# Second stage of a hybrid layer pair: all eight PSUM banks in one pool, and first loads issued one stage earlier

## The chip, the cores and the metric

The kernel runs on one core of one Trainium2 chip. The metric is the device time of one execution in microseconds (us), the median of three runs; less is better. Everything is float32, with float32r (a replicated, reduced form of float32 that TensorE takes at full rate) in the large projections.

## The reference, cut to what matters

Two blocks run one after the other on 2048 positions of width 1024. The first block is where most of the change lies:

```python
def hybrid_layer(x, ...):
    p = rmsnorm(x, norm_g) @ w_in                       # one projection, 3076 columns
    p_shift, g_rwkv, q_down, kv_down, k_idx_raw, w_idx, g_attn = jnp.split(p, ...)
    y_rwkv = rwkv7_branch(p_shift, g_rwkv, ...)         # 8 heads of 64, a recurrence over time
    y_attn = dsa_branch(q_down, kv_down, k_idx_raw, w_idx, g_attn, ...)
    return x + concat(y_rwkv, y_attn) @ w_out

# in dsa_branch, for each block of 128 queries
score = einsum('bqh,bqhs->bqs', wi, relu(einsum('bqhd,bsd->bqhs', qi, k_idx)))   # index scores
_, idx = lax.top_k(score, 256)                          # the 256 best keys of each query
s = einsum('bqhr,bqkr->bhqk', qa, c_kv[idx]);  p = softmax(s);  o = einsum('bhqk,bqkr->bqhr', p, c_kv[idx])
```

The second block is dense attention with 12 heads (queries and keys of 64 plain and 32 rotated features), a small attention to 256 memory rows, gates and an output projection with its residual, and a last normalization.

## The kernel before, in words

**Stages.** The program has seven stages, each with one function for each queue (SP, PE, ACT, DVE, POOL): stage a (normalization, the first projection, the preparation of the recurrence, and the index search of four query blocks), stage 2 (the recurrence of RWKV and the sparse attention with the other searches), the first output projection (`mix1`), stage 4 (the second block's input projection), the heads stage (its head projections and the memory keys), stage 5 (dense attention) and the last output projection (`mix2`). `phase_end` (L342) parts them: each engine drains and signals, and waits for the other compute engines; only SP waits for all. The compute engines don't wait for SP.

**Orders.** In four of the stages the work is a list of pieces (`("score", b, x, n)` is one piece). The code of each engine is run once without a chip, and notes for each piece its waits, its signals and an assumed time for each instruction. `Order.settle` (L202) then plays the engines against each other: each engine has lanes whose pieces stay in order, and it takes the piece that could start first, and among equals the one that stands first in the list. The order that comes out is fixed in the program. On the chip every engine runs its pieces in that order, one by one: whatever stands behind a waiting instruction waits too.

**Stage 2.** It works on two things at once, woven by `weave` (L1415). The RWKV part has 16 turns of 128 positions: `gram` (two products of 64-row blocks), `lv0`, `lvy`, `lvl`, `lvu` (a triangular inverse in five levels, in tiles Xl, Xu, Y, Lm), `sm`, `sa`, `sb`, `sc` (the state's step), `gn0` to `gn2` (group normalization). The attention part has `kT` and `vv` (keys and values), `log` (index scores), `bit` and `flip` (a search for the 256th largest score, 31 steps for each block), `score`, `exp`, `pT` (the probabilities turned by TensorE), `pv`, `rb` and `fin`. Query blocks are taken in the order `BLOCKS` = (7, 6, 5, 4, 15, ..., 8, 3, 2, 1, 0); the first four are searched in stage a and their masks go out to DRAM and come back.

**PSUM in stage 2.** Each of the eight banks has a fixed use. Banks 4, 5 and 6 are a ring (`ring`, L1418): every `kT`, `vv`, `log`, `score` and `pT` piece gets the next one or two of them in the order of the list, and waits for the bank's last reader. Banks 0 and 1 hold `gram`, then `lvl` and `lvu`. Bank 2 holds `lv0`, `lvy`, `gn0`, `gn1`, `gn2` in turn (`b2_free`, L1436). Bank 3 holds the state's step, `sm` to `sc`. Bank 7 holds the attention's output of one pair of heads, from the first `pv` to `fin`:

```python
ring.setdefault(k, []).append((bank[4 + ring_n % 3], ring_last[ring_n % 3]))   # L1418 ff.
ring_last[ring_n % 3] = w
ring_n += 1
```

**Loads at the borders of stages.** `sp_a` (L768) issues at the piece of gate tile (7, 3) the loads of the latents, their two weights and the index keys (`ckvT`, traced as P, `pt`, `kidx`) for stage 2, into memory that the projection has left. All other loads of stage 2 are issued by `sp_2` (L1497) once `phase_end` has passed. `sp_heads` (L2732) issues the loads of head 0, first half (`load_heads(q, 0)`, L3054) for stage 5; `sp_5` (L3110) issues the second half, `load_heads(q, 1)`, after its border. ACT begins stage 5 with four instructions that zero rows of two query tiles (`zero_row`, L3091); a row of maxima, `mrow`, is later put in their place by DMA (`row_in`, L3079).

**Names of the profile.** L134 is `mm`, L137 `turn`, L144 and L145 `act`, L148 `tt`, L154 and L155 `ts`, L160 `stt`, L163 `copy`, L180 `addmax`, L128 `dma`. All eight banks bear the name psum.

## Time and profile before

| | us |
|---|---|
| median of three runs | 4168.22 (4159.9 to 4170.84) |
| the profiled execution, device time | 4170.54 |
| its span, first to last instruction | 4168.7 |
| mean granted TensorE clock | 0.970 |

| engine | busy us | share of the span |
|---|---|---|
| TensorE (PE) | 3868.3 | 93% |
| VectorE (DVE) | 2706.6 | 65% |
| ScalarE (ACT) | 2078.9 | 50% |
| GpSimd (POOL) | 1276.1 | 31% |

The last instruction of TensorE's part of stage a starts at 811.4 us; its first of stage 2 at 816.0, of `mix1` at 2022.1, of the heads stage at 2607.1, of stage 5 at 2822.8. Idle time is shown with what ended it, the last signal that came. The granted clock is given as a share of full speed.

### The profile page before, as it was taken

To read this page: it belongs to the slowest core of one execution; us is meant where nothing else is said; L and a number is where in the kernel's file an instruction comes from. 1 tells how busy PE (TensorE), PEld (TensorE's weight loads), DVE (VectorE), ACT (ScalarE), POOL (GpSimd) and SP (SyncE) were. 2 spreads that over 40 slices of the span, in tenths; PEclk is the share of its full clock that TensorE was granted. 3 is DMA by queue.
4 is the path that set the end of the run, shared out by engine and by line. 5 is a ranking of instruction groups with operands and counts; after the bars stand their busy time and mean duration, and the time that the engine had idled before them with its cause. 6 is when DMAs were issued, how large, how long until landed. Compare 5 with 4: busy or idle time off the path is not lost. (4 is left out here: it accounts for less than half of the span.)

```text
span 4168.7 us, 76113 instructions
## 1 busy us (share of the span) xinstructions
PE 3868.3 (93%) x31032; PEld 2729.3 (65%) x31032; DVE 2706.6 (65%) x5103; ACT 2078.9 (50%) x3089; POOL 1276.1 (31%) x1016
## 2 busy tenths in 40 slices
PE   6999989799888999898898999898999999999899
PEld 5777657566666766666686878774555555555477
DVE  6576778678767777888763332454777777776533
ACT  4354678678677877766333222223333333334421
POOL 2132123233544443553110000002454544545100
PEclk9999999899999999999899999998999999999899
DMA  3344223412211212122565344763232322321243
GB/s 119 93 127 144 83 96 104 144 45 52 59 35 39 54 44 53 44 58 73 162 217 197 109 143 145 251 216 74 58 88 57 79 57 60 86 57 39 94 144 111
DMA packets 389564, 407.29 MB, mean 98 GB/s; under 512 B 115936, under 2 KB 288416, under 8 KB 388960
## 3 DMA queue, kind: packets, MB, share of 16 engines
q1 hardware_dynamic: 388096, 399.00, 32.7%
q8 instruction: 244, 4.00, 0.5%
q10 hardware_dynamic: 1120, 3.45, 0.2%
q14 instruction: 104, 0.85, 0.1%
HBM read 249.87 MB, written 152.47 MB: 97 GB/s over the span
## 5 line engine op out<-in xcount | busy, mean ns | idle before, releaser
L144 ACT ACTIVATE PT<-psum 128x1024 f32<-128x1024 f32 x384 | 394.3, 1027 | 653.5 <-PE psum L134 652.9
L172 DVE TENSOR_REDUCE m<-psum 128x1 f32<-128x1024 f32 x384 | 468.6, 1221 | 286.9 <-PE psum L134 286.9
L134 PE MATMUL psum<-xc,wah 128*128 128x512 f32 x1600 | 528.7, 412 | 15.8 <-DVE xc L148 7.7
L148 POOL TENSOR_TENSOR part<-PT 128x1024 f32<-128x1024 f32 x144 | 341.6, 2372 | 474.3 <-DVE all L148 374.1
L148 POOL TENSOR_TENSOR Lm<-gm,cst 64x512 f32<-64x512 f32 x192 | 258.4, 1346 | 383.3 <-PE psum L134 192.8
L134 PE MATMUL psum<-PT,V 128*64 128x512 f32 x1536 | 371.5, 605 | 0.0
L134 PEld LDWEIGHTS psum<-xc,wah 128*128 128x128 f32 x1600 | 301.6, 192 | 94.5 <-issue 21.6
L134 PE MATMUL psum<-xc,wal 128*128 128x512 f32 x800 | 318.4, 398 | 0.0
L145 ACT ACTIVATE bias<-score,cand,cols 128x2048 bf16<-128x2048 f32 (+4 forms) x155 | 244.5, 1578 | 79.7 <-DVE cand L155 75.9
L145 ACT ACTIVATE sgn<-score,cand,cols 128x1920 bf16<-128x1920 f32 (+4 forms) x155 | 227.9, 1470 | 61.2 <-DVE cand L155 59.7
L134 PE MATMUL psum<-hc,w4h 128*128 128x512 f32 x800 | 249.0, 392 | 0.0
L137 PE MATMUL psum<-cst,P 128*128 128x128 f32 x1088 | 183.6, 293 | 41.8 <-DVE pt L163 27.8
L134 PE MATMUL psum<-m_wh,m_yh 128*128 128x512 f32 x512 | 203.1, 397 | 7.3 <-DVE m_wl L148 5.9
L134 PEld LDWEIGHTS psum<-PT,V 128*64 128x64 f32 x1536 | 93.3, 136 | 178.0 <-issue 177.7
L134 PE MATMUL psum<-m_wl,m_yh 128*128 128x512 f32 x512 | 201.5, 393 | 0.0
L134 PE MATMUL psum<-m_wh,m_yl 128*128 128x512 f32 x512 | 201.4, 393 | 0.0
L180 DVE CUSTOM_DVE_ANT_0 P<-psum,bias 128x512 f32<-128x512 f32 (+3 forms) x320 | 181.9, 605 | 26.9 <-PE psum L134 24.0
L137 PEld LDWEIGHTS psum<-cst,P 128*128 128x128 f32 x1088 | 119.1, 145 | 116.4 <-issue 45.8
L148 DVE TENSOR_TENSOR all<-all,part 128x1024 f32<-128x1024 f32 x144 | 192.1, 1334 | 4.2 <-POOL part L148 4.2
L148 POOL TENSOR_TENSOR all<-PT 128x1024 f32<-128x1024 f32 x48 | 114.6, 2388 | 255.0 <-ACT PT L144 255.0
L134 PE MATMUL psum<-KNh,QNh 64*128 64x512 f32 x768 | 174.6, 451 | 18.5 <-DMA QNh<-scr_qnh 11.4
L134 PEld LDWEIGHTS psum<-KNh,QNh 64*128 64x128 f32 x768 | 72.3, 185 | 181.4 <-DVE m L172 70.9
(391 smaller groups left out, 9038.0 us busy)
## 6 DMA issues: line engine op xcount, KB each, us to landing
raw_a<-in_w_a SPq DMA_DIRECT2D x50, 512.0 KB, 3.7
raw_w<-in_w_in SPq DMA_DIRECT2D x32, 512.0 KB
QNh<-scr_qnh SPq DMA_DIRECT2D x48, 256.0 KB, 4.9
QRh<-scr_qrh SPq DMA_DIRECT2D x96, 128.0 KB, 4.6
QNl<-scr_qnl SPq DMA_DIRECT2D x48, 256.0 KB, 6.2
xin<-in_x SPq DMA_DIRECT2D x16, 512.0 KB
scr_AR<-AR SPq DMA_DIRECT2D x32, 256.0 KB, 2.4
scr_BK<-BK SPq DMA_DIRECT2D x32, 256.0 KB, 2.2
```

The source lines that it names most:

```text
L134: return self.e.matmul(out, a, b, start=start, stop=stop, skip_group_check=True)
L137: return self.e.transpose(out, src, ident) if self.e else self.idle(0.17)
L144: return self.e.activation(out, src, f, bias=bias, scale=scale)
L145: return self.e.activation(out, src, f, bias=bias, scale=scale, accum_out=acc)
L148: return self.e.tensor_tensor(out, a, b, op) if self.e else self.vector(out)
L172: return self.e.tensor_reduce(out, a, AX, op, negate=negate) if self.e else self.vector(a)
L180: return self.e.tensor_tensor_reduce(out, a, b, 1.0, -3.0e38, ALU.add, ALU.max, acc)
```

## The change

In stage 2 no bank has a fixed use any more. A piece that needs banks claims them (`Desk.claim`), and names what will free them. `Order.settle` gives each claim the banks that are free first at the moment at which it places the piece in TensorE's order; a piece whose claim can't be met at all isn't placed yet. In the program the claim becomes a wait for the last reader of just these banks. The order of the banks given in follows from that play. Loads: AR and BK of turn 0 and the index queries of block 4 are now issued by `sp_a` at the piece (7, 3), with waits for their own stores; the tiles of stage 2 are laid out anew so that they fit. `pe_a` ends with a wait for the last two mask stores, and two DVE pieces of stage 2 wait for SP's end of stage a. The masks come back one by one with each block's queries. TensorE waits before the first `score` of a pair for the turned probabilities of two pairs ago and for the block's mask. In the heads stage SP's first piece is given 5 us in the play (no instruction), and SP also issues the high parts of `load_heads(q, 1)`. The zeroing of rows in stage 5 moves from ACT to POOL, and one ACT and one POOL piece wait there for SP's end of the heads stage.

```diff
+    def claim(self, order, k, *frees):
+
+        if self.e is None:
+            self.book.note("claim", frees)
+        return order.banks_of(k, len(frees), self)
...
+    def bank(self, k, n=0):
+        return self.given[k][n][0] if k in self.given else self.banks[n]
+
+    def banks_of(self, k, n, q):
+
+        got = self.given.get(k, [(x, None) for x in self.banks[:n]])
+        for _, free in got:
+            if free:
+                q.wait_ge(*free)
+        return [x for x, _ in got]
...
                     if all(y in at for y in needs):
                         go = max([free[e]] + [at[y] for y in needs])
+                        if claims:
+                            open_ = sorted(empty(n) for n in range(len(used)) if empty(n) is not None)
+                            if len(open_) < len(claims[0]):
+                                continue
+                            go = max(go, open_[len(claims[0]) - 1])
                         if own is None or (go, place[k]) < own[:2]:
                             own = (go, place[k], e, name)
...
+            for y in items:
+                if y[0] == "claim":
+                    some = sorted((empty(n), n) for n in range(len(used)) if empty(n) is not None)[:len(y[1])]
+                    self.given[k] = [(self.banks[n], used[n]) for _, n in some]
+                    for (_, n), x in zip(some, y[1]):
+                        used[n] = x
...
                     if x == 0 and e == 0:
+                        if b == N_EARLY + 1:
+                            q.wait_ge(ended["sp"], 0)
...
                         q.dma(kidx[:, :], scratch["kidx"]).then_inc(*d_kidx.up())
+                        q.wait_ge(d_AR, sub_n[(3, 0, 0)])
+                        q.wait_ge(d_BK, sub_n[(3, 0, 0)])
+                        load_inverse(q, 0)
+                        for m in (4, 5):
+                            n = qqs.index((nth(N_EARLY) // 4, m))
+                            q.wait_ge(d_qo[n % 2], n)
+                        load_index_query(q, N_EARLY)
...
+            for e in range(2):
+                q.wait_ge(d_ebo[e], early.blocks[-2 + e])
...
-        turns_2 = Order(order_2, lane_2)
+        turns_2 = Order(order_2, lane_2, [bank[i] for i in (4, 5, 6, 0, 1, 2, 7, 3)])
+        late.banks = lambda q, k: q.claim(turns_2, k, *[(x_act,) + k + (e,) for e in range(2)])
...
-            for b in early.blocks:
-                N = 128 * (nth(b) + 1)
-                q.dma(bias_of(b)[:, 0:N], scratch["bias"][early.no[b]][:, 0:N]).then_inc(*d_eb.up(b))
             for k in q.pieces(turns_2):
                 what = k[0]
+                if what == "qd" and k[1] < N_EARLY:
+                    b = k[1]
+                    N = 128 * (nth(b) + 1)
+                    q.dma(bias_of(b)[:, 0:N], scratch["bias"][early.no[b]][:, 0:N]).then_inc(*d_eb.up(b))
...
                     q.wait_ge(i_pool, "lm", i, lv)
-                    q.wait_ge(*b2_free[k])
                     if lv == 1:
                         q.wait_ge(i_act, "xl", i)
                     else:
                         q.wait_ge(i_dve, "xl", i, lv - 1)
+                    o, = q.claim(turns_2, k, (i_act, "y", i, lv))
...
                     b, x, n = k[1:]
                     w = width(b, n)
+                    if n == 0:
+                        b0, x0 = pairs_ago(b, x)
+                        q.wait_ge(t_pe, "pT", b0, x0, last_of.get(b0, 0), 1)
+                        bias_there(q, b)
                     q.wait_ge(d_qd[b % 2], b)
                     q.wait_ge(x_act, "kT", x, n)
+                    o = q.claim(turns_2, k, *[(t_dve,) + k + (e,) for e in range(2)])
...
                     b, x, n, e = k[1:]
                     w = width(b, n)
-                    (o, free), = ring[k]
                     q.wait_ge(t_act, "exp", b, x, e)
-                    q.wait_ge(*free)
+                    o, = q.claim(turns_2, k, (pt_copy(k),) + k)
...
                     if n == 0:
-                        q.wait_ge(t_dve, "y", *pairs_ago(b, x, 1))
+                        q.claim(turns_2, k, (t_dve, "y", b, x))
+                    o = turns_2.bank(("pv", b, x, 0))
...
         def sp_heads(q):
             for k in q.pieces(turns_h):
+                if k == ("c2", 0):
+                    q.idle(5.0)
...
                         load_heads(q, 0)
+                        for c in (1, 2):
+                            for what in ("qn", "qr"):
+                                m = eh_use[(what, c, 0)]
+                                q.wait_ge(d_eh[m % 5], m)
+                        load_heads(q, 1, "h")
...
+            rows, ones = QRl[i][ps, :].rearrange("p (n t) -> p n t", n=8), rep(one[ps, :], 8)
+            if q.name == "pool":
+                return q.ts(rows, ones, 0.0, None, ALU.mult)
+            return q.act(rows, ones, ACT.Copy, scale=0.0)
...
-                    load_heads(q, k[1])
+                    load_heads(q, k[1], "l" if k[1] == 1 else "hl")
...
-            for i in (1, 2):
-                for a in range(2):
-                    t = zero_row(q, i, a)
-            t.then_inc(*q_act.up("zero"))
...
+                    if g == 3:
+                        q.wait_ge(ended["sp"], 4)
...
         def pool_5(q):
+            for i in (1, 2):
+                for a in range(2):
+                    zero_row(q, i, a).then_inc(*q_pool.up("zero", i, a))
+                    q.wait_ge(q_pool, "zero", i, a)
...
+                    if g == 2:
+                        q.wait_ge(ended["sp"], 4)
```

## Rows read from the trace of the kernel before

**Rows 1.** The page's part 1, busy time of each engine.

```profile
PE 3868.3 (93%) x31032; PEld 2729.3 (65%) x31032; DVE 2706.6 (65%) x5103; ACT 2078.9 (50%) x3089; POOL 1276.1 (31%) x1016
```

**Rows 2.** Busy time by stretch: us, then busy us (and count) of PE, PEld, DVE, ACT, POOL, granted clock, DMA share, GB/s.

```profile
811.80:850.00 38.20, 26.01 (x108) 10.61 (x108) 15.30 (x21) 9.09 (x16) 11.61 (x12) 0.73 0.72 203
850.00:1990.00 1140.00, 1027.63 (x15935) 744.59 (x15933) 877.58 (x2523) 846.40 (x1229) 501.56 (x418) 0.97 0.20 49
1990.00:2016.20 26.20, 17.98 (x106) 11.47 (x104) 12.55 (x70) 5.70 (x24) 0.00 (x0) 0.60 0.39 111
...
2615.00:2650.00 35.00, 26.55 (x97) 20.12 (x96) 18.33 (x26) 11.45 (x18) 1.49 (x4) 0.85 0.95 343
...
2820.00:2870.00 50.00, 30.71 (x175) 19.54 (x175) 15.88 (x14) 13.83 (x15) 9.41 (x4) 0.76 0.43 101
2870.00:3880.00 1010.00, 1009.83 (x6786) 569.23 (x6782) 731.92 (x684) 385.67 (x376) 504.31 (x235) 1.00 0.27 63
```

**Rows 3.** TensorE's groups of instructions, 850 to 1990: busy, mean ns, idle before and releasers.

```profile
L137 PE MATMUL psum<-cst,P 128*128 128x128 f32 x1072 | 178.4, 292 | 40.6 <-DVE pt L163 27.2 <-DVE mx L180 7.4 <-ACT P L145 3.8
L134 PE MATMUL psum<-kT,qd 64*128 64x512 f32 (+3 forms) x620 | 174.2, 599 | 3.2 <-DVE mx L180 2.6 <-ACT rl L144 0.4
L134 PE MATMUL psum<-pt,vv 128*64 128x128 f32 x2136 | 154.9, 289 | 18.1 <-DVE pt L163 10.7 <-ACT pt L144 4.4 <-DVE gate L148 2.9
L134 PE MATMUL psum<-Xl,Lm 64*64 64x64 f32 x2560 | 94.0, 224 | 9.5 <-DVE yc L160 3.3 <-POOL Lm L148 2.6 <-issue 2.1
...
L134 PE MATMUL psum<-kidx,qx 64*128 64x512 f32 (+3 forms) x220 | 66.9, 604 | 6.0 <-ACT rl L144 3.6 <-DVE mx L180 2.1 <-DVE pt L163 0.3
L134 PE MATMUL psum<-ar,bk 64*128 64x128 f32 x480 | 35.1, 283 | 4.9 <-DVE Xu L148 2.7 <-DVE gm L148 2.3
```

**Rows 4.** TensorE's timeline, and the busy time by stretch, around the longest wait for a bank.

```profile
1468.90 0.69 PE L137 MATMUL psum<-cst,P 128*128 128x128 f32 x2 [5.04 <-DVE pt L163]
...
1460.00:1470.00 10.00, 4.96 (x57) 3.77 (x55) 6.22 (x14) 3.19 (x6) 7.48 (x6) 0.82 0.28 79
```

**Rows 5.** TensorE's waits (times, longest), 1985 to 2016.

```profile
PE psum L134 <- DVE gate L148: 6.1, 5, 2.3
```

**Rows 6.** TensorE's timeline at the start of stage 2.

```profile
816.03 3.75 PE L134 MATMUL psum<-P,pt 128*128 128x512 f32 x4 [4.22 <-POOLq L189]
...
825.74 2.08 PE L134 MATMUL psum<-kidx,qx 64*128 64x512 f32 x4 [3.20 <-DMA qx<-scr_q]
831.52 2.08 PE L134 MATMUL psum<-ar,bk 64*128 64x128 f32 x16 [3.70 <-DMA bk<-scr_BK]
```

**Rows 7.** SP's waits, 815 to 835, and the busy time of one stretch.

```profile
SPq L116 <- DMA scr_bias<-xtmp: 3.6, 1, 3.6
...
816.00:818.00 2.00, 1.97 (x3) 0.97 (x4) 0.00 (x0) 0.00 (x0) 0.31 (x1) 0.50 0.95 383
```

**Rows 8.** The timeline of TensorE and ACT at the start of the heads stage.

```profile
2618.80 1.09 PE L134 MATMUL psum<-krr,sel 64*128 64x512 f32 x2 [3.22 <-DVE krr L148]
...
2633.04 0.80 PE L134 MATMUL psum<-cch,wqh 128*128 128x512 f32 x1 [5.20 <-DVE el L148]
...
2630.63 1.06 ACT L145 ACTIVATE V<-V 128x1024 f32<-128x1024 f32 x1 [9.20 <-DMA V<-in_mem]
```

**Rows 9.** The timeline of TensorE and ACT at the start of stage 5.

```profile
2836.35 0.80 PE L134 MATMUL psum<-KNh,QNh 64*128 64x512 f32 x2 [11.41 <-DMA QNh<-scr_qnh]
2838.64 0.79 PE L134 MATMUL psum<-KS,QRh 64*128 64x512 f32 x2 [1.49 <-DMA QRh<-scr_qrh]
...
2858.17 0.50 PE L134 MATMUL psum<-KNh,QNh 64*128 64x512 f32 x2 [0.86 <-DVE m L172]
...
2865.04 0.50 PE L134 MATMUL psum<-KNh,QNh 64*128 64x512 f32 x2 [0.87 <-DVE m L172]
...
2822.94 4.26 ACT L144 ACTIVATE QRl<-cst 32x1024 fp32r<-32x1024 f32 x4 [0.19 <-issue]
```

**Rows 10.** One of GpSimd's groups in stage 2.

```profile
L155 POOL TENSOR_SCALAR bias<-rl 128x512 bf16<-128x512 f32 (+3 forms) x30 | 52.4, 1748 | 2.7
```

More of the change, by code:

```diff
@@ L213, in settle, with empty @@
         free, table, at = {e: 0.0 for e in lanes}, {e: "exp" for e in lanes}, {}
+        used = [None] * len(self.banks)
+        def empty(n):
+            x = used[n]
+            return 0.0 if x is None else at.get((id(x[0]), x[1:]))
         self.by = {e: [] for e in lanes}
@@ L520, in index_act @@
                         q.wait_ge(*I.rl_free[k][e])
-                    q.act(I.relu(k, e)[:, 0:w], I.ring[k][e][0][:, 0:w], ACT.Relu).then_inc(*I.x_act.up("log", b, n, x, e))
+                    q.act(I.relu(k, e)[:, 0:w], I.bank(k, e)[:, 0:w], ACT.Relu).then_inc(*I.x_act.up("log", b, n, x, e))
             elif what == "sel0":
@@ L734, in program @@
             if k[0] == "log":
-                early.ring[k] = [(bank[4 + e], early_last[e]) for e in range(2)]
+                early.ring[k] = list(early_last)
                 early_last = [(early.x_dve, "acc") + k[1:] + (e,) for e in range(2)]
@@ L745, in program, with early_banks @@
                 early.junk_free[b] = [(n_act, "sq", NT - 1), (n_act, "xh", NT - 1, 0), (n_dve, "xl", NT - 1, 0)]
+        def early_banks(q, k):
+            for free in early.ring[k]:
+                q.wait_ge(*free)
+            return bank[4], bank[5]
+        early.banks = early_banks
         subs = [(hp, c, s) for half_ in range(2) for hp in range(4) for c in (2 * half_, 2 * half_ + 1) for s in range(2)]
@@ L1424, in program @@
             what = k[0]
-            who = {"kT": [(x_act, "kT") + k[1:]], "vv": [(x_dve, "vv") + k[1:]], "log": [(x_act,) + k + (e,) for e in range(2)],
-                   "score": [(t_dve,) + k + (e,) for e in range(2)]}.get(what, [])
-            if what == "pT":
-                who = [(pt_copy(k),) + k]
-            for w in who:
-                ring.setdefault(k, []).append((bank[4 + ring_n % 3], ring_last[ring_n % 3]))
-                ring_last[ring_n % 3] = w
-                ring_n += 1
             if what in ("log", "sel2"):
@@ L1444, in program @@
         fins = [k[1:] for k in dsa_order if k[0] == "fin"]
-        late.ring, late.rl_free = ring, rl_free
+        late.rl_free = rl_free
         late.score, late.cols, late.cand, late.flip = score, colsv, cand, flip
@@ L1497, in sp_2, with load_index_query @@
+        def load_index_query(q, b):
+            a = late.ago(b, 2)
+            if a >= 0:
+                q.wait_ge(x_pe, "log", a, last_of[a], 1)
+            q.dma(qx[b % 2][:, :, :], feat("q")[:, 4:6, 128 * nth(b):128 * nth(b) + 128]).then_inc(*d_qx[b % 2].up(b))
         def sp_2(q):
-            for b in early.blocks:
-                N = 128 * (nth(b) + 1)
-                q.dma(bias_of(b)[:, 0:N], scratch["bias"][early.no[b]][:, 0:N]).then_inc(*d_eb.up(b))
             for k in q.pieces(turns_2):
@@ L1533, in sp_2 @@
                     b = k[1]
-                    a = late.ago(b, 2)
-                    if a >= 0:
-                        q.wait_ge(x_pe, "log", a, last_of[a], 1)
-                    q.dma(qx[b % 2][:, :, :], feat("q")[:, 4:6, 128 * nth(b):128 * nth(b) + 128]).then_inc(*d_qx[b % 2].up(b))
+                    if b > N_EARLY:
+                        load_index_query(q, b)
                 elif what == "qd":
@@ L1688, in pe_2 @@
                     i = k[1]
-                    q.wait_ge(*b2_free[k])
+                    last = {"gn0": "yc", "gn1": "gv", "gn2": "yn"}[what]
+                    o, = q.claim(turns_2, k, (s_dve, last, i))
                     if what == "gn0":
                         q.wait_ge(s_dve, "ys", i, 1)
-                        q.mm(bank[2], blk, ys[:, :, :]).then_inc(*s_pe.up("gn0", i))
+                        q.mm(o, blk, ys[:, :, :]).then_inc(*s_pe.up("gn0", i))
                     elif what == "gn1":
@@ L1880, in dve_2 @@
                     q.wait_ge(x_pe, "vv", x)
-                    q.copy(vv[:, x, :], ring[k][0][0]).then_inc(*x_dve.up("vv", x))
+                    q.copy(vv[:, x, :], turns_2.bank(k)).then_inc(*x_dve.up("vv", x))
                 elif what in INDEX:
@@ L1918, in dve_2 @@
                             q.wait_ge(t_pe, "pv", *pv_at[m - 2])
-                        q.copy(pt[m % 2][:, e, 0:w], ring[k][0][0][:, 0:w]).then_inc(*t_dve.up("pT", b, x, n, e))
+                        q.copy(pt[m % 2][:, e, 0:w], turns_2.bank(k)[:, 0:w]).then_inc(*t_dve.up("pT", b, x, n, e))
                     if n == 0 and e == 1:
@@ L3060, in load_heads @@
             for part, K, d_k, Qn, d_n, Qr, d_r in (("h", KNh, d_knh, QNh, d_qnh, QRh, d_qrh), ("l", KNl, d_knl, QNl, d_qnl, QRl, d_qrl)):
+                if part not in parts:
+                    continue
                 if e == 0:
```

195 lines of the change are left out of this document (93 added, 102 removed).

## The prediction, made before the change was built or run

> **What bounds the kernel now.** I read the page's part 1 first: TensorE is busy for 3868.3 of 4168.7 us [rows 1], so time can come only from its gaps, from its slow clock, or from less work. The change takes no matmul away. The busy time by stretch then says where gaps and slow clock lie [rows 2]. Stage 5 after 2870 has none (1009.83 of 1010 us, clock 1.00). The body of stage 2, 850 to 1990, has 1140 - 1027.6 = 112.4 us of idle at a granted clock of 0.97; its last 26.2 us are busy for 18.0 at 0.60; its first 38.2 us for 26.0 at 0.73. The heads stage's first 35 us and stage 5's border have 8.4 and 19.3 us of idle at 0.85 and 0.76. VectorE, at 877.6 of 1140 us, and ScalarE at 846.4 are the next in the body [rows 2]. The lines of TensorE in the body tell what ended its idle time [rows 3].
>
> **The body of stage 2.** What the pool can take away is a wait for a bank, not one for data. By the code, a `pT` piece that waits for DVE `pt` or `P` (the mx of L180) waits for the ring's last reader: 27.2 + 7.4 us. In the same way 2.6 + 0.4 at `score`, 3.6 + 2.1 + 0.3 at `log`, 3.3 at Xl,Lm (bank 2, held by `gn0`), 4.9 at ar,bk (banks 0 and 1), 2.9 at `pv` (bank 7). The sum is 54.7 us [rows 3]. The other 57.7 us are waits for data (`pv` for the copied probabilities, 10.7 + 4.4; the inverse for Y, Xu and Lm), which the change leaves. Of the 54.7 not all goes: where VectorE is late with a copy, TensorE gets past the bank and meets the same copy a little later as data of `pv`, since the SBUF tile `pt` still has two buffers. Nothing excludes either end: 0 if VectorE's lateness is all of it, 54.7 if it is only the ring. I take half, 27, since with five more banks a late reader must be later by several pieces, and VectorE has 262 us of idle here to catch up.
>
> The clock gives more back. The mean of 0.97 over 1140 us is 34 us of full-speed time lost. The longest wait for a bank, 5.04 us, stands in a stretch with a clock of 0.82 [rows 4]: TensorE had stood still, then it ran on at 1.2 GHz instead of 2.4. Not all of these stretches follow a bank wait, so between 0 and 34 I take 13, somewhat over a third.
>
> The new waits: TensorE now waits for the mask and the turned probabilities of two pairs ago before it claims for `score`. All its later pieces stand behind, the inverse too. VectorE waited for the same before it read; I put it at 0, at most 2 us, as the order is worked out with it. The masks' loads, moved behind on SP to each block's queries, have the same cover; 0.
>
> **The last 26 us.** Pairs of small blocks go through bank 7 one after the other: 6.1 us of waits for the gate's last reader [rows 5], and 18.0 us of work at 0.60. With other banks for the next pair the wait goes in part (3 of 6.1, since softmax, copy and `pv` of a pair stay a chain), and a higher clock gives perhaps 3. Together 6, between 0 and 6.1 + 7.2 = 13.
>
> **The first 38 us.** Removed are TensorE's waits for the index queries (3.20) and for BK (3.70) [rows 6], 6.9 us. Added is TensorE's wait for the last mask store. This one is on the path: behind it stand the end of TensorE's stage, and so the start of all compute engines. SP was 3.6 us behind that store's issue at 815.8 before, so it landed at 819.7 [rows 7]. Now it stands on SP's queue behind 1.18 MB more (AR and BK with 512 KB each, index queries with 128), at 383 GB/s [rows 7] 3.1 us, so about 822.8, and TensorE begins at 823 instead of 816.0 [rows 6]. It then has ready what it waited for: 7.0 later against 6.9 saved. Net 0; from 4 gained (if the loads don't delay the store) to 5 lost. DMA: Bandwidth & Descriptors in the Trainium skill (Queues, rings and completion order) speaks against this part: each DMA engine takes up its queue in order, and a signal lands only after all earlier writes of that engine. By it the store can't overtake the loads and TensorE begins at 823; if it could, it would begin near 820 and the 4 us of the other bound would be gained. That 3.6 us passed for a store of 160 KB fits the rule, but doesn't show it.
>
> **The start of the heads stage.** ScalarE waits 9.20 us for the memory rows with `eh` behind it, and TensorE waits 5.20 and 3.22 us [rows 8]. Told that SP is 5 us later, the order should put `eh` first and the memory rows behind. I take 5 of the 8.4; 0 if the same wait comes elsewhere, 10 with the clock.
>
> **The border of stage 5.** TensorE stood 11.41 + 1.49 us for QNh and QRh of the second half [rows 9]; now they are loaded before the border. What is late next? VectorE's maxima: a group with three passes of maxima repeats every 2865.04 - 2858.17 = 6.87 us at full clock [rows 9]. After the standstill TensorE ran on at 0.5: 50 us from 2820 have a mean of 0.76, 12 us lost, of which most falls on idle time; I count 4. So 11.4 + 1.5 + 4 = 16.9. Off go about 1 for a row of maxima that still comes by DMA: 16, between 10 and 20. The six added loads delay SP's stores of `eh` by six issues; five buffers cover that. ScalarE is rid of 4.26 us of zeroing ahead of the first exponential [rows 9]. GpSimd does a row of 512 in 1748 ns [rows 10], so four of 1024 in about 14 us; its cover is that it has no other work before the first sums, and that the next query tiles are needed only after eight groups, some 50 us. Uncovered it would be up to 14 us. The waits for SP's end fall before their pieces are due.
>
> **The sum.** 27 + 13 + 6 + 0 + 5 + 16 = 67 us. The profiled execution took 4170.5; it becomes 4103.5. It lies 2.3 us above the median of the runs, which is less than their spread, so I forecast 4103.
>
> **The rivals.**
> (1) The waits only change their name. In the body nothing is gained: TensorE passes `pT` and stands at `pv` for VectorE's copy, and the clock dips stay. For it: 15.1 us of idle at `pv` are of this kind already, and one VectorE order serves all lanes. Against it: five more banks, and 34.6 us at `pT` alone. It gives 6 at the end, 5 and 16: 4170.5 - 27 = 4143. TensorE: Matmul & The Clock Gate in the Trainium skill, under HAM oscillation, reports that double-buffered PSUM gave its kernel no further gain; by that, this rival holds. The trace bears it out for the waits at `pv` alone, since those at `pT` name a reader of a bank.
> (2) The common pool starves the inverse, and the kernel is slower. Banks 0 to 2 were the inverse's own; its waits for them were only 3.3 + 4.9 us [rows 3]. Now a claim names the bank that was first free in the play, and on the chip TensorE stands at that bank even if others are empty, with the whole queue behind it. A stall as long as the longest today (5.04, and 1.8 us of clock for a stretch at 0.82 [rows 4]) in each of 16 turns is 109 us. It replaces the 54.7, whereas nothing of the clock or the end is gained: body +54, less 21 at the other borders, 4204. It decides from ten such stalls on, the 67 us of the forecast. Against it: a bank freed earliest has the most slack, and VectorE isn't full.
> (3) The order gets better by itself. Lanes were chained through the ring in the list's order and are now free. All of 54.7, 26 of the 34, 10 at the end, 21 at the borders: 4170.5 - 112 = 4059.
> (4) The change doesn't do what it says: the play still puts the pieces so that the same few banks matter, and the border of stage 5 gains its idle time back as a wait for the row of maxima. Then within 12 us of before, 4165.
>
> **How the numbers follow.** The forecast has 0.55, (1) 0.20, (2) 0.11, (3) 0.10, (4) 0.04. The bounds of the body (0 to 54.7 and 0 to 34) make the forecast's own range 4070 to 4135. To hold the time 8 times in 10 the range must take in (3) and (1) with their spread: 4050 to 4158; outside are (2), most of (4), and the edges. A measurement of this kernel can tell about 0.3%, 12.5 us. Faster by more: nearly all of the forecast, (1) and (3), 0.83. Same: (4) and the upper edge of (1), 0.06. Slower: 0.11.
>
> **What the profile after would show.** In the body, the idle before cst,P ended by DVE `pt` falls from 27.2 to under 15 while that before pt,vv rises by less; a mean clock of 0.98 or more; the body shorter by some 40 us. At stage 2's start, a first matmul near 823 and then no wait for a DMA. At stage 5's border, no 11.4 us. The forecast is wrong if pt,vv takes over the idle time (1), if Xl, Y and Xu groups show waits for VectorE's or ScalarE's readers of other lanes (2), or if TensorE's start of stage 2 slips beyond 825.

## The result and the profile after

The changed kernel takes 4096.52 us (median; 4093.37 to 4107.78), the one before 4169.47 beside it: ratio 0.9833, 95% interval 0.9821 to 0.9845, so 73 us faster. The prediction was 4103, with a range of 4050 to 4158. The profiled execution took 4093.37 us; its span is 4091.6, 77.1 less than before. From the marks of TensorE's timeline (the first matmul of each part), this difference splits as follows:

| part | before, us | after, us | difference | predicted |
|---|---|---|---|---|
| stage a, to TensorE's last matmul | 811.8 | 808.4 | -3.4 | 0 |
| standstill at the border to stage 2 | 4.2 | 13.2 | +9.0 | +7 |
| stage 2, to `mix1`'s first matmul | 1206.1 | 1131.2 | -74.9 | -53 |
| `mix1` and stage 4 | 585.0 | 582.9 | -2.1 | 0 |
| heads stage | 215.7 | 224.5 | +8.8 | -5 |
| stage 5, to the attention to the memory rows | 1056.3 | 1042.9 | -13.4 | -16 |
| that attention and `mix2` | 289.6 | 288.5 | -1.1 | 0 |

Stage a ended anywhere from 808.4 to 817.4 in the kernels of this study (line by line it is nearly the same program in all of them), so 3.4 us there are scatter, and a median is not to be explained to the microsecond from one trace.

Part 1 of the page of the changed kernel (against [rows 1]):

```profile
PE 3821.8 (93%) x31032; PEld 2718.7 (66%) x31032; DVE 2683.9 (66%) x5103; ACT 2069.3 (51%) x3085; POOL 1279.6 (31%) x1020
```

The number of matmuls is the same, but TensorE is busy for 46.5 us less. That is more than half of the gain, and the prediction looked for it only as clock. Its busy time by stretch (columns as in [rows 2]; the border, the first 28 us, the body and the end of stage 2, the start of the heads stage, the border and the rest of stage 5):

```profile
808.40:821.60 13.20, 0.03 (x1) 0.00 (x0) 1.58 (x4) 0.60 (x1) 2.95 (x5) 0.59 0.90 266
821.60:850.00 28.40, 28.12 (x129) 11.31 (x129) 17.45 (x25) 12.96 (x23) 5.75 (x5) 0.95 0.53 135
850.00:1923.00 1073.00, 978.30 (x15892) 731.61 (x15890) 851.57 (x2505) 835.37 (x1217) 494.77 (x417) 0.97 0.21 52
1923.00:1946.90 23.90, 18.73 (x128) 11.88 (x126) 14.23 (x80) 6.65 (x28) 3.43 (x5) 0.65 0.52 144
2535.50:2580.00 44.50, 32.18 (x128) 25.29 (x129) 21.55 (x30) 15.27 (x22) 1.48 (x4) 0.85 0.79 284
...
2757.00:2807.00 50.00, 42.42 (x263) 26.19 (x261) 24.35 (x23) 15.35 (x16) 24.20 (x10) 0.90 0.37 90
...
2810.00:3870.00 1060.00, 1043.33 (x7055) 591.47 (x7051) 755.45 (x752) 413.75 (x474) 500.64 (x234) 0.99 0.29 68
```

TensorE's groups in the body of stage 2, 850 to 1923 (against [rows 3]; helpers stand six lines lower now, L134 is L140, L163 is L169, L180 is L186):

```profile
L143 PE MATMUL psum<-cst,P 128*128 128x128 f32 x1066 | 165.7, 286 | 5.2 <-ACT P L151 2.5 <-DVE mx L186 1.1 <-DVE pt L169 0.8
L140 PE MATMUL psum<-kT,qd 64*128 64x512 f32 (+3 forms) x616 | 154.2, 589 | 9.1 <-DVE mx L186 3.5 <-POOL bias L161 2.0 <-issue 1.4
L140 PE MATMUL psum<-pt,vv 128*64 128x128 f32 x2128 | 150.9, 284 | 23.1 <-DVE pt L169 13.7 <-DVE sm L175 6.7 <-ACT pt L150 1.3
L140 PE MATMUL psum<-Xl,Lm 64*64 64x64 f32 x2560 | 93.6, 223 | 15.3 <-DVE Xl L154 3.8 <-POOL Lm L154 3.8 <-issue 3.4
...
L140 PE MATMUL psum<-kidx,qx 64*128 64x512 f32 (+3 forms) x208 | 51.9, 580 | 6.8 <-DVE gm L154 3.3 <-DVE mx L186 2.2 <-DVE gate L154 1.0
L140 PE MATMUL psum<-ar,bk 64*128 64x128 f32 x480 | 34.5, 283 | 0.9 <-DVE gm L154 0.6 <-DVE mx L186 0.2
```

The idle time ahead of the turns (cst,P) fell from 40.6 to 5.2 us, its part for DVE `pt` from 27.2 to 0.8. At `pv` (pt,vv) the idle time rose from 18.1 to 23.1 only, over the whole change; how much the pool alone renames is read from the bound banks below. And the two groups that go in pairs of row halves, `score` (kT,qd) and `log` (kidx,qx), are busy for 35 us less together (174.2 + 66.9 against 154.2 + 51.9), though their counts fell by only 16 of 840 in this window (worth some 4 us).

TensorE's timeline at the two places where it stands longer than before, the border to stage 2 and the start of the heads stage:

```profile
821.63 3.36 PE L140 MATMUL psum<-P,pt 128*128 128x512 f32 x4 [13.21 <-DMA scr_bias<-xtmp]
824.92 1.13 PE L140 MATMUL psum<-kidx,qx 64*128 64x512 f32 x4
...
2567.75 0.80 PE L140 MATMUL psum<-cch,wqh 128*128 128x512 f32 x1 [12.11 <-DVE el L154]
```

And SP's queue before the second of them:

```profile
2549.05 6.90 SPq L134 DMA_DIRECT2D V<-in_w_mem  x8
2555.99 1.17 SPq L134 DMA_DIRECT2D scr_qnh<-eh  x1
```

The 13.21 us end with the last mask store, as predicted, and the first index matmul behind it waits for nothing. The 12.11 us are put down to DVE `el`, but behind that stands ScalarE's sixth `eh` tile, whose buffer is free only when the first `eh` store has landed:

```profile
2566.30 0.60 ACT L150 ACTIVATE eh<-psum 128x512 fp32r<-128x512 f32 x1 [5.14 <-DMA scr_qnh<-eh]
```

SP issues that store only after ten loads of memory rows and weights, as before.

### The profile page after: what moved, and what is told of

Read it like the earlier page. It is cut to its first block and busy times, and to the rows that moved or that the text cites. A ratio compares the mean times of both kernels' runs of the same rounds, so it can differ in the third digit from the quotient of the medians.

```text
span 4091.6 us, 76338 instructions
## 1 busy us (share of the span) xinstructions
PE 3821.8 (93%) x31032; PEld 2718.7 (66%) x31032; DVE 2683.9 (66%) x5103; ACT 2069.3 (51%) x3085; POOL 1279.6 (31%) x1020
## 5 line engine op out<-in xcount | busy, mean ns | idle before, releaser
L140 PE MATMUL psum<-xc,wah 128*128 128x512 f32 x1600 | 525.9, 410 | 13.9 <-DVE xc L154 7.7
L140 PE MATMUL psum<-PT,V 128*64 128x512 f32 x1536 | 371.5, 605 | 0.0
L140 PEld LDWEIGHTS psum<-xc,wah 128*128 128x128 f32 x1600 | 300.1, 191 | 92.1 <-issue 21.8
L140 PE MATMUL psum<-xc,wal 128*128 128x512 f32 x800 | 317.3, 397 | 0.0
L140 PE MATMUL psum<-hc,w4h 128*128 128x512 f32 x800 | 248.4, 392 | 0.0
L140 PEld LDWEIGHTS psum<-PT,V 128*64 128x64 f32 x1536 | 93.3, 136 | 177.9 <-issue 177.6
L140 PE MATMUL psum<-m_wh,m_yh 128*128 128x512 f32 x512 | 203.3, 397 | 7.3 <-DVE m_wl L154 5.9
L140 PE MATMUL psum<-m_wl,m_yh 128*128 128x512 f32 x512 | 201.7, 394 | 0.0
L140 PE MATMUL psum<-m_wh,m_yl 128*128 128x512 f32 x512 | 201.4, 393 | 0.0
L186 DVE CUSTOM_DVE_ANT_0 P<-psum,bias 128x512 f32<-128x512 f32 (+3 forms) x320 | 180.7, 605 | 23.1 <-PE psum L140 22.7
L140 PEld LDWEIGHTS psum<-KNh,QNh 64*128 64x128 f32 x768 | 72.4, 185 | 171.8 <-DVE m L178 70.9
L140 PE MATMUL psum<-pt,vv 128*64 128x128 f32 x2176 | 157.2, 286 | 27.9 <-DVE pt L169 13.7
L140 PE MATMUL psum<-KNh,QNh 64*128 64x512 f32 x768 | 173.9, 450 | 9.9 <-DVE m L178 9.7
L151 ACT ACTIVATE P<-P,mx 128x1024 f32<-128x1024 f32 (+15 forms) x128 | 152.3, 1191 | 51.1 <-DVE mx L178 51.1
L143 PE MATMUL psum<-cst,P 128*128 128x128 f32 x1088 | 171.5, 288 | 5.2 <-ACT P L151 2.5
```

What stands on the lines that cost most here:

```text
L140: return self.e.matmul(out, a, b, start=start, stop=stop, skip_group_check=True)
L143: return self.e.transpose(out, src, ident) if self.e else self.idle(0.17)
L151: return self.e.activation(out, src, f, bias=bias, scale=scale, accum_out=acc)
L186: return self.e.tensor_tensor_reduce(out, a, b, 1.0, -3.0e38, ALU.add, ALU.max, acc)
```

## The experiments

Differences of a few microseconds are read from stage lengths in the traces, since they hardly show in ratios with intervals of this width. Where several kernels have the same order in stage 2, that stage agrees to about 3 us: it takes 1131.2 us in the changed kernel, and 1131.9, 1131.0 and 1134.1 in the three below that leave its order alone. All ratios are against the kernel before.

**Both waits ahead of the pair.** Theory: a bank wait between the two row halves costs their overlap. The edit, shown for `score` and made for `log` too:

```diff
-                    for e in range(2):
-                        o, free = ring[k][e]
-                        q.wait_ge(*free)
+                    for _, free in ring[k]:
+                        q.wait_ge(*free)
+                    for e in range(2):
+                        o = ring[k][e][0]
```

> The kernel before, with one edit: where a score or log piece takes two banks of the ring, TensorE waits for both ahead of its first matmul, instead of for the second bank between the two matmuls (rows 0 to 63 and rows 64 to 127 of the array). Nothing else changes; number of banks, order and data are those of before. Theory P (a wait between the two halves costs their overlap): in the changed kernel TensorE's busy time for these two groups fell by 34 us of the whole run (score 179.0 to 158.5, log 74.2 to 60.8). If the wait in the middle is the cause, most of that comes here as well, busy time of the two groups falls by 20 to 34 us, and the kernel gets 15 to 30 us faster. Rival (the 34 us came only of the higher clock and of free banks): the groups' busy time stays within 5 us of before, the time within 8 us; it could even lose a little, as the first matmul now waits for the later of two readers.

Ratio 1.0002 (0.9991 to 1.0013): no effect. Groups of its body, 850 to 1993:

```profile
L137 PE MATMUL psum<-cst,P 128*128 128x128 f32 x1072 | 178.5, 292 | 39.8 <-DVE pt L163 26.8 <-DVE mx L180 7.2 <-ACT P L145 3.8
L134 PE MATMUL psum<-kT,qd 64*128 64x512 f32 (+3 forms) x620 | 163.1, 602 | 15.5 <-DVE mx L180 10.8 <-ACT rl L144 1.8 <-DVE pt L163 1.4
L134 PE MATMUL psum<-pt,vv 128*64 128x128 f32 x2136 | 155.1, 289 | 17.7 <-DVE pt L163 10.3 <-ACT pt L144 4.4 <-DVE gate L148 2.7
...
L134 PE MATMUL psum<-Xu,Y 64*64 64x64 f32 x2560 | 91.9, 222 | 5.4 <-ACT Y L144 5.4
L134 PE MATMUL psum<-Y,Xu 64*64 64x64 f32 x2048 | 76.1, 226 | 7.8 <-ACT Y L144 6.6 <-DVE Xu L148 1.0
L134 PE MATMUL psum<-kidx,qx 64*128 64x512 f32 (+3 forms) x220 | 58.5, 606 | 14.5 <-DVE mx L180 9.3 <-ACT rl L144 4.6 <-ACT kT L144 0.4
```

Each expectation is half right. The busy time of the two paired groups (kT,qd and kidx,qx) does fall, by 11.1 + 8.4 = 19.5 us [rows 3], but the idle time rises by 12.3 + 8.5 = 20.8, and nothing is gained. A group's busy time counts overlapping instructions once, so these 19.5 us were no work: they were waits for the second bank that lay under the first half's busy time. The theory of lost overlap falls as a cause, and the body held about 20 us more of bank waits than the idle column showed.

**Masks' loads moved.** The edit before, and SP loads each early mask ahead of its block's queries, not all at the start of stage 2 (the `for b in early.blocks` loop moves to the piece `qd`).

> The kernel before with both bank waits ahead of the pair (4170.7) and one more edit: on SP the loads of the early blocks' masks no longer stand first in stage 2 but go ahead of each block's queries, as in the changed kernel. In the runs with late first loads TensorE waited for no DMA after the border, though AR, BK and the index queries were not loaded early; so I hold that the masks' loads ahead of them made it wait, not the lateness of the loads. If so, the waits for qx and bk (6.9 us) go here as well and the time falls by 5 to 9 us, to 4162 to 4166. Whatever stage 2 doesn't gain here of the 48 us between this kernel and the one with bound banks and late loads (stage 2: 1208.7 against 1160.5) is due to the freedom of the order. Rival: no change (4167 to 4175), and all 48 us are the order's, the start included.

Ratio 0.9995 (0.9984 to 1.0006): no effect. TensorE's waits from 812 to 850:

```profile
PE psum L134 <- DMA bk<-scr_BK: 4.0, 1, 4.0
PE psum L134 <- DMA qx<-scr_q: 1.2, 1, 1.2
```

They are 5.2 us against 6.9 [rows 6]. The masks' loads were not what made TensorE wait there, and the expectation was wrong.

**The added wait at the scores.** The edit of the first experiment, and the two waits that the change puts ahead of each pair's first `score`.

```diff
+                    if n == 0:
+                        b0, x0 = pairs_ago(b, x)
+                        q.wait_ge(t_pe, "pT", b0, x0, last_of.get(b0, 0), 1)
+                        bias_there(q, b)
```

> The kernel before with both bank waits ahead of the pair (stage 2: 1208.7 us) and one more part of the change: TensorE's score piece first waits for the mask and for the turned probabilities of two pairs ago, so that it takes its two ring banks only when VectorE can empty them at once. The ring of three banks stays, and the banks stay chained in the order of the list. It splits the 48 us between this kernel and the one with bound banks and late loads (stage 2: 1160.5). If scores that were issued too early had held ring banks for nothing, stage 2 falls by 20 us or more, to under 1190 (kernel under 4152). If it is the freedom of the lanes to take a bank in any order, stage 2 stays within 6 us of 1208.7 (4165 to 4177), and the 48 us are that freedom's. A loss (over 1215) would mean that the wait holds up the pieces behind it.

Ratio 1.0014 (1.0003 to 1.0025), stage 2 at 1215.7 us against 1208.7 without the wait: a small loss. Scores issued too early were not what blocked the ring, as long as its banks are chained in the order of the list.

**Bound banks, with early and with late loads.** Here the play still hands out the banks, but each kind of piece may only take those that it had before.

```diff
+        def banks_for(k):
+            return {"gram": (3, 4), "lvl": (3,), "lvu": (4,), "lv0": (5,), "lvy": (5,), "gn0": (5,), "gn1": (5,), "gn2": (5,),
+                    "pv": (6,), "sm": (7,)}.get(k[0], (0, 1, 2))
```

> The changed kernel, but the claims of stage 2 may only take the banks that each kind had before: three for the ring (score, log, kT, vv, pT), one each for the two inverse outputs, one shared by the first level and the normalisation, one for pv, one for the small ones, two for gram (shared with the inverse). The order freedom (banks given out as the orders are worked out), both claims ahead of the pair, and the early loads stay. If the number of banks open to a waiting piece is what pays (the forecast's reason: 27 us of waits and 13 of clock), most of 40 us is lost again: 4125 to 4140. If it is the pairing and the freer order, it stays within 15 us of the changed kernel: 4097 to 4112. Idle time before cst,P (5.2 after, 40.6 before) tells the two apart: over 25 in the first case, under 15 in the second.

> The changed kernel with the banks of stage 2 bound to their old kinds (as in the run with fixed banks, 4129.1) and with the first loads issued in stage 2 again. Against the kernel before (waits for both banks ahead of the pair: 4170.7) it leaves of stage 2's change only that banks are given out while the orders are worked out, so that a piece of another lane may come first. If this freedom is what the 41 us between those two runs come from, this one stays within 6 us of 4129. If the early loads were behind a good part of it, it goes to 4137 or more.

Ratios 0.9902 (0.9879 to 0.9925) and 0.9884 (0.9865 to 0.9903), medians of 4129.12 and 4122.87 us. With early loads the result is where the first theory had it, 33 us above the changed kernel; but it is also 43 us below the kernel before, and so the banks that a piece may choose from are less than half of the gain. The body with bound banks and early loads, 850 to 1957, is the one to hold against the changed kernel's:

```profile
L143 PE MATMUL psum<-cst,P 128*128 128x128 f32 x1068 | 172.4, 290 | 31.0 <-DVE pt L169 24.2 <-ACT P L151 3.6 <-DVE mx L186 1.6
L140 PE MATMUL psum<-kT,qd 64*128 64x512 f32 (+3 forms) x620 | 162.4, 599 | 24.4 <-ACT rl L150 10.3 <-DVE mx L186 7.8 <-DVE pt L169 3.5
L140 PE MATMUL psum<-pt,vv 128*64 128x128 f32 x2136 | 152.6, 285 | 8.7 <-DVE gate L154 6.7 <-DVE pt L169 1.0 <-ACT pt L150 0.7
```

From here to the free pool the idle time ahead of the turns and of `score` falls by 25.8 + 15.3 = 41.1 us, but that of `pv` rises by 14.4 (8.7 to 23.1): about a third of these waits does come back under another name. Stage 2 takes 1164.9 us here, of which TensorE is idle for 121.3, against 1131.2 and 106.1; so the pool's 34 us are 15 of idle time and 18 of busy time. They hold more than the choice of a bank, since the play also puts TensorE's pieces in another order once any bank will do.

With late loads it is 6 us faster still, just outside of what either theory allowed and away from the one that credited the early loads. The groups of the body with late loads, 850 to 1955:

```profile
L143 PE MATMUL psum<-cst,P 128*128 128x128 f32 x1072 | 171.2, 289 | 39.8 <-DVE pt L169 27.1 <-DVE mx L186 6.5 <-ACT P L151 3.2
...
L140 PE MATMUL psum<-pt,vv 128*64 128x128 f32 x2136 | 151.9, 285 | 7.2 <-DVE gate L154 3.5 <-DVE pt L169 2.5 <-ACT pt L150 1.1
...
L140 PE MATMUL psum<-Xu,Y 64*64 64x64 f32 x2560 | 91.0, 221 | 0.8 <-ACT Y L150 0.8
L140 PE MATMUL psum<-Y,Xu 64*64 64x64 f32 x2048 | 74.2, 222 | 6.5 <-ACT Y L150 6.5
```

Against the rows of the first experiment, the waits for the ring ahead of the turns are all still there (39.8 in both). What went are waits for data: `pv` from 17.7 to 7.2, the inverse's Xu,Y and Y,Xu from 5.4 + 7.8 to 0.8 + 6.5; and none for a DMA is left behind the border. Stage 2 takes 1160.5 us, 48 less than with the ring's chain and both waits first (1208.7), 34 of them idle time (154.1 to 120.2) and 14 busy time. Of what lies between the two kernels I tried the moved masks (nothing) and the score waits (a loss) one at a time. What is left is that the banks are no longer chained in the order of the list, so that the play may put another lane first. TensorE's order does differ: 14 matmuls stand ahead of the first index matmul instead of 6. The new layout of the tiles and VectorE's two waits for SP were not tried by themselves, nor the score waits without the chain. So the 48 us are the order's by elimination.

**Six and five banks.** The pool is shortened to its first six or five banks; nothing is bound to a kind.

> The changed kernel with six banks in the pool of stage 2 instead of eight; nothing is bound to a kind. If pooling alone does it and eight are more than needed, within 8 us of the changed kernel (4097 to 4105). If the count of banks matters, the waits for banks come back in part: 4110 to 4130. If a common pool can starve the inverse (the rival of the prediction), it should show here first: idle time before the groups of Xl, Xu and Y rises from 29.5 to over 60, and the time goes over 4150.

> The changed kernel with five banks in the pool of stage 2. Stage 2 took 1131.2 us with eight and 1138.4 with six, against 1164.9 with eight banks bound to their kinds and 1206 before. If the pool gets short at some count (the prediction's rival of a starved inverse), two banks are held for long times by the small products and by pv, so that three are left for all others: stage 2 then takes 1170 to 1220, with idle time before Xl, Xu and Y over 60 us. If pooling bears even this, it stays under 1155.

Ratios 0.9851 (0.9825 to 0.9878) and 0.9914 (0.9900 to 0.9927); stage 2 takes 1138.4 and 1170.8 us against 1131.2 with eight. The turns in the body with six banks, then with five:

```profile
L143 PE MATMUL psum<-cst,P 128*128 128x128 f32 x1064 | 170.4, 288 | 20.8 <-DVE pt L169 6.7 <-ACT P L151 4.0 <-DVE mx L186 3.0
```

```profile
L143 PE MATMUL psum<-cst,P 128*128 128x128 f32 x1040 | 166.0, 287 | 37.2 <-DVE pt L169 15.7 <-DVE mx L186 7.5 <-DVE ys L169 4.0
...
L140 PE MATMUL psum<-Xu,Y 64*64 64x64 f32 x2560 | 93.2, 224 | 8.1 <-DVE pt L169 2.6 <-DVE iv L161 2.0 <-DVE gate L154 1.1
L140 PE MATMUL psum<-Xl,Lm 64*64 64x64 f32 x2560 | 92.3, 222 | 10.1 <-POOL Lm L154 4.7 <-DVE Xl L154 2.6 <-DVE Xu L154 2.2
L140 PE MATMUL psum<-Y,Xu 64*64 64x64 f32 x2048 | 75.5, 225 | 8.1 <-ACT Y L150 6.4 <-DVE pt L169 1.2 <-DVE mx L186 0.5
```

Six free banks beat eight bound ones by 26.5 us of stage 2 (1164.9 to 1138.4), and the last two give 7.2, by one trace each. Five lose 32 us against six, as expected; but it isn't the inverse that starves (8.1 + 10.1 + 8.1 = 26.3 us of idle time, where over 60 was expected), it is the turns again.

**Late first loads, and stores first.** AR and BK of turn 0 and the index queries go back to stage 2; or they stay in stage a but behind the last mask store.

```diff
-                        load_inverse(q, 0)
...
-                        load_index_query(q, N_EARLY)
```

> The changed kernel, but the first inverse's operands and the first late index query (1.18 MB) are again loaded from stage 2 and not from the end of the stage in front. Read from the two traces: in the changed kernel TensorE stands 13.2 us at this border (8.8 to 9.4 more than before) and then waits for no DMA; before, it stood 4.2 us and then 3.2 and 3.7 for DMAs. If the early loads hold up the mask store, the border goes back to about 4 to 6 us of standstill, TensorE's waits for qx and bk (7 us) come back, and the kernel lies within 4 us of the changed one (4093 to 4101), a little better or worse. If the early loads are a gain, as their place in the change suggests, it is 5 to 9 us slower. If the standstill stays at 13 us, it is the other waits added at this border (TensorE and others for the mask stores) that cause it.

> The changed kernel with one block of SP's instructions moved: the early loads are issued right behind the last mask store instead of ahead of it. Theory (the store lands late because 1.18 MB of loads stand ahead of it in the queues): SP's wait for that store falls from 6.8 us to about 3.6, TensorE begins stage 2 about 3 us earlier against the end of its previous stage, and waits for bk or qx stay under 4 us; the kernel is 0 to 4 us faster than the changed one. Rival (the store is late for another reason): the 13 us of standstill stay.

Ratios 0.9808 (0.9785 to 0.9831) and 0.9818 (0.9799 to 0.9837). SP's wait for the mask store with late loads, then with the store ahead of the loads:

```profile
SPq L116 <- DMA scr_bias<-xtmp: 3.8, 1, 3.8
```

```profile
SPq L116 <- DMA scr_bias<-xtmp: 1.0, 1, 1.0
...
PE psum L140 <- DMA scr_bias<-xtmp: 8.9, 1, 8.9
PE psum L140 <- DMA qx<-scr_q: 0.5, 1, 0.5
```

With the early loads ahead of the store SP waited 6.8 us for it. The border is 8.6 and 8.9 us long instead of 13.2: the loads ahead of the store cost TensorE 4.5 us. Three of them are the longer wait for the landing (6.8 against 3.8). The rest is SP's own queue: it issues the store 5.4 us after TensorE's last matmul of stage a in the changed kernel (at 813.83) and 4.0 us after it with late loads (at 817.80), since the loads' issues stand ahead. On the longer landing, DMA: Bandwidth & Descriptors in the Trainium skill (Queues, rings and completion order) has each DMA engine take up its queue in order, and the 6.8 against 3.8 us agree with it. But TensorE's waits for BK and the index queries don't come back when the loads are late, against what was expected. The 6.9 us were saved by the order, which puts more key and value products first; the early loads bought nothing. With late loads stage 2 itself is 4.4 us shorter too (1126.8, and 1129.3 in the last kernel below, which has the same order; bound banks gave 4.4 as well). TensorE's order is another one there, with 14 matmuls instead of 4 ahead of the first index matmul; whether that is the reason isn't shown. With the store first the total is only 1.5 us better than the changed kernel's, inside the scatter.

**The heads stage.** In the first kernel the 5 us in the play are left out and the second half's high parts are loaded in stage 5; in the second the memory rows wait for the fifth tile:

```diff
                 elif k[0] == "mload":
+                    q.wait_ge(h_act, "eh", 4)
```

> The changed kernel without its edits in the heads stage: SP isn't told of 5 us of idle time ahead of the memory rows' loads, and the second half's queries are loaded in stage 5 again instead of at the end of the heads stage. Stage 2 is that of the changed kernel. If stage 5's border gave the 13.4 us by which that stage got shorter, and the heads stage's 8.8 us came of these edits, stage 5 takes 1056 again and the heads 216, so the kernel is 3 to 7 us slower than the changed one: about 4101. If the heads' loss has another cause (what stage 2 leaves behind), the heads stay at 224 and the kernel goes to about 4110.

> The changed kernel with one wait added on SP: the ten loads of the memory rows wait for ScalarE's fifth copied tile, so that the stores of the first tiles are issued ahead of them. In the changed kernel TensorE stands 12.1 us near the start of the heads stage for a tile whose buffer waits for such a store; before it was 8.4 us. If the stores behind the loads are the cause, the heads stage takes 216 to 220 us instead of 224.5, and the kernel is 4 to 9 us faster than the changed one (4088 to 4093). If it is only the additional loads at the end of that stage, it stays at 222 or more.

Ratios 0.9845 (0.9821 to 0.9870) and 0.9807 (0.9788 to 0.9827). Without the heads' edits the stage takes 215.1 us, and TensorE stands at stage 5 again:

```profile
2775.64 0.79 PE L140 MATMUL psum<-KNh,QNh 64*128 64x512 f32 x2 [14.33 <-DMA QNh<-scr_qnh]
2777.84 0.80 PE L140 MATMUL psum<-KS,QRh 64*128 64x512 f32 x2 [1.41 <-DMA QRh<-scr_qrh]
```

From stage 5's first matmul to the end of the span it takes 14.3 us longer than the changed kernel (1345.7 against 1331.4). So the two edits gain 14.3 from stage 5 on and pay 9 in the stage in front. With `eh` stores ahead of the memory loads that stage takes 218.2 us, and its longest standstill is 3.7:

```profile
PE psum L140 <- DVE el L154: 3.7, 1, 3.7
PE psum L140 <- DVE rot L154: 1.8, 1, 1.8
```

About 6 of the 9 us are the stores' place; the other 3 fit 3.63 us for DVE `m` and 1.22 for a DMA of `QRh` that appear near the end of the stage where the second half is loaded.

**All three mended.** Late first loads, `mload` behind the fifth tile, and no wait for the mask stores at the end of TensorE's stage a.

```diff
-            for e in range(2):
-                q.wait_ge(d_ebo[e], early.blocks[-2 + e])
```

> The changed kernel with three edits: the first loads of stage 2 are issued in stage 2 again, the memory rows' loads wait for the fifth tile of the heads stage, and TensorE doesn't wait for the last mask store at the end of its stage. By the single runs: late loads gave 4.5 us at the border and as much in stage 2, the heads stage 6, and the wait is 4.4 us of what is left of the standstill at the border (8.6 against 4.2 before). If these add up: 4076 to 4084, a border of 4 to 5 us and a heads stage of 218 us. Rival: without the wait TensorE begins at the same moment, since something else ends only then (the border stays at 8 us, 4082 to 4088).

4076.72 us, ratio 0.9779 (0.9766 to 0.9793): the fastest of the study, 20 us under the changed kernel. The start of its stage 2:

```profile
814.38 6.18 PE L140 MATMUL psum<-P,pt 128*128 128x512 f32 x8 [4.22 <-POOLq L195]
820.39 2.74 PE L140 MATMUL psum<-pt,P 128*128 128x512 f32 x6
823.06 2.85 PE L140 MATMUL psum<-kidx,qx 64*128 64x512 f32 x12
```

The border is 4.2 us again, and TensorE does 9 us of key and value products before it needs the index queries; none of its later starts in the first 36 us waits for a DMA. The rival (something else ends only then) falls. This prices the wait for the mask stores at 4.4 us (8.6 to 4.2); whether the new layout of tiles needs it (these stores read tiles of stage a, whose memory stage 2 takes over), no run shows.

## Why the prediction held, and where it didn't

**The body (27 for waits, 13 for the clock).** The mechanism is right in the main, and rival (1), by which the body gains nothing, is refuted: with the pool the idle time ahead of the turns falls from 31.0 (bound banks, early loads) to 20.8 (six) to 5.2 (eight), and `pv` takes over 14.4 us of it and of the scores', not all. TensorE: Matmul & The Clock Gate in the Trainium skill (HAM oscillation) tells of a kernel to which double-buffered PSUM gave no more; here the pool gave 34 us of stage 2 (1164.9 to 1131.2), and the measurement decides. The sizes were off in three ways. First, only what stood in the idle column was summed; 20 us more of bank waits lay in busy time. Second, the step "The other 57.7 us are waits for data", "which the change leaves", failed: freeing the chain let the play move lanes past each other, and this took mostly waits for data. It is the largest single part, 48 us of stage 2, and the prediction had it only as rival (3) with a chance of 0.10. Third, idle and busy fell together: stage 2 lost 28.4 us of idle time (134.5 to 106.1) and 46.4 of busy time (1071.6 to 1025.2), of which 17 were waits in disguise (1071.6 to 1054.6 in the first experiment). That the 28.4 lie so near to the 27 is luck: the pool gave only 15 of idle time and the freed order 34, of which 20 had first come over from busy time when both waits went ahead. Of the remaining 29 of busy time the clock accounts for about half. TensorE's busy time by stretch (us, busy and count, granted clock, DMA share, GB/s) in the kernel before, and then after:

```profile
850.00:1100.00 250.00, 232.29 (x3533) 0.97 0.18 44
1100.00:1400.00 300.00, 260.87 (x4045) 0.97 0.19 46
1400.00:1700.00 300.00, 273.73 (x4256) 0.94 0.19 46
1700.00:1990.00 290.00, 260.75 (x4114) 0.98 0.23 60
```

```profile
850.00:1100.00 250.00, 234.38 (x3692) 0.99 0.20 49
1100.00:1400.00 300.00, 272.79 (x4548) 0.98 0.21 49
1400.00:1700.00 300.00, 268.63 (x4396) 0.98 0.20 50
1700.00:1923.00 223.00, 202.50 (x3272) 0.95 0.23 61
```

Lost time by these rows (1 less the clock, times the stretch) is 7.5 + 9 + 18 + 5.8 = 40.3 before and 2.5 + 6 + 6 + 11.2 = 25.7 after: 15 us, against 13 predicted; the clock is given to 0.01, which is some 5 us over the body. It rose in the middle (0.94 to 0.98) and fell at the end (0.98 to 0.95). The other half of the 29 stays open. The paired groups are again among them: from the first experiment to the changed kernel they fell from 163.1 + 58.5 to 154.2 + 51.9, 15.5 us, some 4 of it by their counts; whether that is more hidden waits isn't shown.

**The last 26 us (6).** The waits for the gate's reader [rows 5] went, and 4.6 us for DVE `sm` came; 18.73 us of work at 0.65 in 23.9. About 2 instead of 6 (26.2 us to 23.9): the 4.6 us for `sm` fit the chain inside a pair, which the prediction named.

**The start (0).** The +7 of standstill was +9.0, ended by the very store. But "It then has ready what it waited for" gave the early loads a gain that the order makes without them. The clock of the first stretch also rose, from 0.73 over 38.2 us [rows 2] to 0.95 over 28.4, or 10.3 to 1.4 us lost by the same sum, of which part falls on idle time. Against late loads the early ones cost 4.5 us.

**The heads stage (-5).** It came out at +8.8. The step that failed is "the order should put `eh` first and the memory rows behind". ScalarE's order did put five `eh` tiles first; SP's did not change, since its loads were merely told late and not made to wait for anything. So TensorE ran five tiles ahead, until it hung on the first buffer's store, behind ten loads. The 5.20 us [rows 8] became 12.11. The prediction also set "six issues; five buffers cover that" for the added loads; the 3 us that the stores' place doesn't explain fit them.

**Stage 5 (-16).** 13.4 by the marks, 14.3 against the kernel without the edit. The standstills of 11.41 and 1.49 us [rows 9] are gone, the first 50 us run at 0.90 instead of 0.76, and GpSimd's zeroing stayed covered. TensorE waited 1.1 us there for the DMA of the row of maxima, for which the prediction took off about 1.

**Rival (2)** did not occur with eight banks, nor in its own form with five. The forecast's own range, "4070 to 4135", isn't what its bounds give: 0 to 54.7 and 0 to 34 for the body, with 27 for the rest, make 4055 to 4143; the measured time lies in both. The sum came near (67 us against 73 of the medians) partly by luck: 20 us too little for stage 2 with its border, and 14 too hopeful in the heads stage.

## What to carry to other kernels

When buffers are given out while the order is worked out, look for two gains and not one: fewer waits for a buffer, and lanes that are no longer tied to each other by the list; here the second was the larger. An early load isn't free if a store that someone waits for stands behind it, and telling a planner that an engine is late doesn't move its work: make the loads wait for what should go first. A wait that is gone at one group may stand at the next one, so compare the length of the stage. Before you sum the idle column, look for waits that stand between two overlapping instructions, where they are counted as busy time.

## What the hardware showed that was not expected

A wait between the two row halves of a 64-row matmul pair (rows 0 to 63 and 64 to 127) shows as busy time. The mean of one instruction stayed the same (599 and 602 ns), but the group's busy time fell from 174.2 to 163.1 us and its idle time rose from 3.2 to 15.5 when both waits were put ahead: two halves that lie under each other take 11 us less together, and the time returns as visible idle time. For a change of waits, the length of a stage is therefore a safer measure than its idle time.
